# The causal convolution of x in rows: shifted copies by DMA and VectorE products in place of transposes and column taps

## The chip, the cores and the metric

The kernel runs on one NeuronCore of one Trainium2 chip. The metric is device time in microseconds (us) of one launch. The engines are TensorE (PE, its weight loads PEld), VectorE (DVE), ScalarE (ACT), GpSimd (POOL) and SyncE (SP), which here issues nearly all DMAs. Each runs its own instruction stream in order; semaphores join them.

## The reference

One decoder layer over 256 tokens of width 2048 in float32. The part around the change is the Mamba-2 branch (`w_in` gives `z`, `xbc` and others from the normed input):

```
xbc = silu(causal_depthwise_conv(xbc, conv_w, conv_b))   # 4 taps along the tokens
xs, Bm, Cm = split(xbc)                                  # xs: 4096 channels, 64 heads of 64
xdt = xs * dt
y = (C B^T * decay) @ xdt (+ the part over the first 128 tokens, scaled by exp(a_cs))
y = y + d_skip * xs
y = rms_norm_per_512_channels(y * silu(z)) * norm_w
```

Channel c of the convolution at token s is `conv_b[c] + sum over back=0..3 of conv_w[3-back, c] * xbc[s-back, c]`, with zeros in front of token 0. The rest of the layer (differential attention, gates, output projection, SwiGLU) is not touched.

## The kernel before

Tokens lie on the partitions as two tiles of 128 rows (`TT = 2`). Every weight matrix passes through one ring of four buffers in *units* of 256 x 512 weights: SP loads a unit (`load`, L410), ScalarE rounds it to `w_hi` (`split_hi`, L724), VectorE computes the remainder `w_lo = w_raw - w_hi` (`split_lo`, L1257), and TensorE does 12 matmuls of 512 columns on it (`rows_unit`, L2246). ScalarE and VectorE are four units ahead of TensorE: the unit that they call u of a chunk is TensorE's u + 4. ScalarE may round unit n only when TensorE has done unit n-4, because of the ring. A *chunk* is eight units, 512 output columns.

The Mamba-2 stage walks over eight groups of 512 channels. Each group has an x chunk (sum in `acc[0]`) and a z chunk (sum in `acc[1]`). All the other work of the stage is written by hand into the order of the units: `between(u)` on TensorE, and `x_chunk`, `z_chunk` on ScalarE and VectorE, with a number u at each step. The order of one group:

- ScalarE copies the x chunk's sum to rows `x_proj` (L965).
- TensorE, z chunk after u = 0: eight transposes of `x_proj` into `acc[0]`, the matmuls of C and B (L2596), and eight transposes of the former group's `y_row`.
- ScalarE does the first tap and the bias into `conv_x` (four instructions, L838), with channels on the partitions; VectorE adds the other three taps (twelve instructions, L1447) and frees `acc[0]`; ScalarE takes the silu (L995).
- ScalarE, u = 2 and 3: `exps`, eight exponentials each (L977), which waits for masks that GpSimd adds (L2193); VectorE, u = 3 and 4: `decays` (L1658).
- TensorE, z chunk after u = 4: eight transposes of `conv_x` back to rows; VectorE, u = 5: `xdt` and `xdt_end`; ScalarE copies the rows to `y_row` (L1002), GpSimd multiplies them by `d_skip` (L2199).
- TensorE, next x chunk: after u = 1 `y_products` (32 small matmuls of `decay` and `xdt`), after u = 3 `y_rows`. VectorE, u = 3: `tail_gated`; ScalarE, u = 4: squares; GpSimd: reciprocal root; VectorE, u = 6: `tail_normed` (L1624); u = 1 of the z chunk: `tail_transposed` (L1630).

The first group has no former group, and the last group's tail lies in the first two of four gate chunks that follow.

Of the kernel before, what the change touches and what calls it, by code (L numbers as in the profile page):

```python
# [28 lines left out]
ALU = mybir.AluOpType  # L29
# [3 lines left out]
P = 128  # L33
T = 256
# [150 lines left out]
def layer(nc, x, mix_norm_w, w_in, conv_w, conv_b, dt_bias, a_log, d_skip, ssm_norm_w, w_ssm_proj,  # L185
# [3 lines left out]
    with ctx:  # L189
# [6 lines left out]
        def sem(name):  # L196
# [77 lines left out]
        conv_x = at("conv_x", 191, [P, CT, T])  # L274
# [66 lines left out]
        conv_first, conv_done = sem("conv_first"), sem("conv_done")  # L341
        sq_read = sem("sq_read")
        bc_rows_ready, bc_T, x_rows_ready, x_T = sem("bc_rows_ready"), sem("bc_T"), sem("x_rows_ready"), sem("x_T")
# [14 lines left out]
        xs_ready, xs_T, xdt_ready, xrow_ready, skip_ready = (sem(n) for n in (  # L358
            "xs_ready", "xs_T", "xdt_ready", "xrow_ready", "skip_ready"))
# [39 lines left out]
        def _(sp):  # L399
# [302 lines left out]
        def _(act):  # L702
# [232 lines left out]

            def tail_columns(g):
# [4 lines left out]
            def x_chunk(g, head):  # L941
                for u in range(UPC):
                    split_hi()
                    if u == 1 and not head:
                        tail_columns(g - 1)
# [8 lines left out]
                    if u == 4 and not head:  # L954
# [26 lines left out]
            def z_chunk(g, head):  # L981
                for u in range(UPC):
                    split_hi()
                    if u == 0:

                        act.wait_ge(x_T, g + 1)
                        for n in range(CT):
                            last = conv_first_taps(sums(0)[:, n], g * CT, conv_x[:, n], n)
                        last.then_inc(conv_first, 1)
# [27 lines left out]
            for c in range(4):  # L1017
                for u in range(UPC):
                    split_hi()
                    if c == 0 and u == 1:  # L1020
                        tail_columns(G - 1)
                    if c == 0 and u == 4:
# [1791 lines left out]
```

## Time and profile before

| | us |
|---|---|
| three runs, median (lowest to highest) | 2051.03 (2051.0 to 2053.92) |
| the profiled execution | 2051.72 |
| its span | 2050.1 |
| TensorE busy in the span | 2040.8 |
| VectorE, ScalarE, GpSimd busy | 1566.3, 1172.0, 171.6 |

A span runs from the first to the last instruction. Times in rows count from the span's start. The eight groups' x and z chunks lie between about 592 and 998 us. A matmul's busy time includes its pipeline's depth, so matmuls that follow each other overlap in the profile.

### The profile page before, as it was taken

To read this page: it belongs to the slowest core of one execution; us is meant where nothing else is said; L and a number is where in the kernel's file an instruction comes from. 1 tells how busy PE (TensorE), PEld (TensorE's weight loads), DVE (VectorE), ACT (ScalarE), POOL (GpSimd) and SP (SyncE) were. 2 spreads that over 40 slices of the span, in tenths; PEclk is the share of its full clock that TensorE was granted. 3 is DMA by queue.
4 is the path that set the end of the run, shared out by engine and by line. 5 is a ranking of instruction groups with operands and counts; after the bars stand their busy time and mean duration, and the time that the engine had idled before them with its cause. 6 is when DMAs were issued, how large, how long until landed. Compare 5 with 4: busy or idle time off the path is not lost.

```text
span 2050.1 us, 28075 instructions
## 1 busy us (share of the span) xinstructions
PE 2040.8 (100%) x9580; PEld 1677.7 (82%) x9580; DVE 1566.3 (76%) x1861; ACT 1172.0 (57%) x1496; POOL 171.6 (8%) x195
## 2 busy tenths in 40 slices
PE   9999999999999999999999999999999999999999
PEld 8888877778888888888888888888888888887887
DVE  6777866665856777777667887888898889877866
ACT  5444655555556666666655554556666666645543
POOL 1121000000011222222000000010000000000000
PEclk9999999999999999999999999999999999999999
DMA  7656675654566666666565657598888888667574
GB/s 250 199 182 203 188 220 166 176 162 152 182 204 186 185 185 184 185 190 187 167 192 183 212 168 238 177 307 244 258 254 237 250 259 250 196 205 232 176 246 154
DMA packets 220626, 419.80 MB, mean 205 GB/s; under 512 B 16449, under 2 KB 22002, under 8 KB 220290
## 3 DMA queue, kind: packets, MB, share of 16 engines
q1 hardware_dynamic: 212162, 399.48, 61.8%
q0 software_dynamic: 7776, 18.94, 4.4%
q8 instruction: 47, 0.77, 0.2%
q10 hardware_dynamic: 608, 0.34, 0.1%
q14 instruction: 33, 0.27, 0.0%
HBM read 410.25 MB, written 4.26 MB: 202 GB/s over the span
## 4 chain that ended last, share of the span: by engine, by line
PE 92%; DVE 3%; DMA 2%; ACT 1%; issue 0%; SPq 0%; DVEq 0%; ACTq 0%
PE acc L2246 72%; PE side L2333 8%; PE acc L2333 6%; PE side L2262 3%; DMA w_raw<-in_w_ffn_down 1%; DVE w_lo L2038 1%; PE side L2402 1%; PE side L2549 1%; DVE w_raw L1953 0%; ACT w_hi L1216 0%; DVE w_lo L1257 0%; DMA x_row<-in_x 0%; DMA w_raw<-in_w_in 0%; PE acc L2262 0%; ACT w_hi L724 0%
## 5 line engine op out<-in xcount | busy, mean ns | idle before, releaser
L1257 DVE TENSOR_TENSOR w_lo<-w_raw,w_hi 128x1024 fp32r<-128x1024 f32 x332 | 420.7, 1280 | 245.7 <-ACT w_hi L724 244.5
L724 ACT ACTIVATE w_hi<-w_raw 128x1024 fp32r<-128x1024 f32 x332 | 348.5, 1057 | 355.7 <-PE acc L2246 315.2
L2246 PE MATMUL acc<-w_hi,h_hi 128*128 128x512 f32 x1248 | 498.7, 400 | 0.2
L2246 PE MATMUL acc<-w_hi,h_lo 128*128 128x512 f32 x1248 | 487.0, 390 | 0.0
L2246 PE MATMUL acc<-w_lo,h_hi 128*128 128x512 f32 x1248 | 485.9, 389 | 0.0
L2246 PEld LDWEIGHTS acc<-w_hi,h_hi 128*128 128x128 f32 x1248 | 234.4, 188 | 52.7 <-issue 7.0
L2246 PEld LDWEIGHTS acc<-w_hi,h_lo 128*128 128x128 f32 x1248 | 234.3, 188 | 50.3
L2246 PEld LDWEIGHTS acc<-w_lo,h_hi 128*128 128x128 f32 x1248 | 234.7, 188 | 47.6 <-issue 1.9
L1932 DVE TENSOR_TENSOR w_lo<-w_raw,w_hi 128x1024 fp32r<-128x1024 f32 x136 | 165.1, 1220 | 38.0 <-ACT w_hi L1137 35.4
L1053 ACT ACTIVATE w_hi<-w_raw 128x1024 fp32r<-128x1024 f32 x110 | 116.6, 1061 | 117.2 <-PE acc L2246 70.2
L1137 ACT ACTIVATE w_hi<-w_raw 128x1024 fp32r<-128x1024 f32 x136 | 142.9, 1057 | 65.8 <-PE acc L2246 50.4
L1216 ACT ACTIVATE w_hi<-w_raw 128x1024 fp32r<-128x1024 f32 x102 | 107.8, 1060 | 106.5 <-DMA w_raw<-in_w_ffn_down 57.4
L1734 DVE TENSOR_TENSOR w_lo<-w_raw,w_hi 128x1024 fp32r<-128x1024 f32 x110 | 132.2, 1223 | 47.3 <-ACT w_hi L1053 45.4
L1137 ACT ACTIVATE w_hi<-side_raw 128x1024 fp32r<-128x1024 f32 x100 | 106.2, 1062 | 98.1 <-PE acc L2246 45.2
L2038 DVE TENSOR_TENSOR w_lo<-w_raw,w_hi 128x1024 fp32r<-128x1024 f32 x102 | 122.6, 1223 | 47.9 <-ACT w_hi L1216 46.8
L2246 PE MATMUL acc<-w_hi,x2T_hi 128*128 128x512 f32 x384 | 150.9, 393 | 0.5 <-DVE w_lo L1932 0.5
L2246 PE MATMUL acc<-w_hi,x2T_lo 128*128 128x512 f32 x384 | 149.6, 389 | 0.0
L2246 PE MATMUL acc<-w_lo,x2T_hi 128*128 128x512 f32 x384 | 149.4, 389 | 0.0
L1932 DVE TENSOR_TENSOR w_lo<-side_raw,w_hi 128x1024 fp32r<-128x1024 f32 x100 | 122.1, 1221 | 18.3 <-ACT w_hi L1137 16.6
L2246 PE MATMUL acc<-w_hi,a_hi 128*128 128x512 f32 x252 | 98.2, 390 | 0.0
L2246 PE MATMUL acc<-w_hi,a_lo 128*128 128x512 f32 x252 | 98.1, 389 | 0.0
L2246 PE MATMUL acc<-w_lo,a_hi 128*128 128x512 f32 x252 | 98.1, 389 | 0.0
(436 smaller groups left out, 3445.9 us busy)
## 6 DMA issues: line engine op xcount, KB each, us to landing
w_raw<-in_w_in SPq DMA_DIRECT2D x320, 512.0 KB, 4.3
w_raw<-in_w_ffn_down SPq DMA_DIRECT2D x88, 512.0 KB, 4.9
w_raw<-in_w_ffn_gate SPq DMA_DIRECT2D x68, 512.0 KB, 4.6
w_raw<-in_w_ffn_up SPq DMA_DIRECT2D x68, 512.0 KB, 5.2
w_raw<-in_w_ssm_proj SPq DMA_DIRECT2D x64, 512.0 KB, 4.4
side_raw<-in_w_ffn_up SPq DMA_DIRECT2D x40, 512.0 KB, 4.7
w_raw<-in_w_attn_proj SPq DMA_DIRECT2D x32, 512.0 KB, 3.7
w_raw<-in_w_out SPq DMA_DIRECT2D x32, 512.0 KB, 4.7
```

Of the source, the lines that this page charges most:

```text
L724: nc.scalar.activation(w_hi[:, r], w_raw[:, n % RING], ACT.Copy).then_inc(hi_ready, 1)
L1053: nc.scalar.activation(w_hi[:, unit.slot % RING], w_raw[:, source], ACT.Copy).then_inc(hi_ready, 1)
L1137: nc.scalar.activation(w_hi[:, unit.slot % RING], ffn_source(names, name), ACT.Copy).then_inc(hi_ready, 1)
L1216: nc.scalar.activation(w_hi[:, unit.slot % RING], w_raw[:, source], ACT.Copy).then_inc(hi_ready, 1)
L1257: nc.vector.tensor_tensor(w_lo[:, r], w_raw[:, n % RING], w_hi[:, r].bitcast(F32), ALU.subtract).then_inc(lo_ready, 1)
L1734: nc.vector.tensor_tensor(w_lo[:, r], w_raw[:, source], w_hi[:, r].bitcast(F32), ALU.subtract).then_inc(lo_ready, 1)
L1932: nc.vector.tensor_tensor(w_lo[:, r], ffn_source(names, names[n]), w_hi[:, r].bitcast(F32), ALU.subtract).then_inc(lo_ready, 1)
L2038: nc.vector.tensor_tensor(w_lo[:, r], w_raw[:, source], w_hi[:, r].bitcast(F32), ALU.subtract).then_inc(lo_ready, 1)
L2246: done = nc.tensor.matmul(acc[p][:, t], a[:, k0 + kk, cut], w[:, r, kk], start=first and kk == n == 0, stop=last and kk == UK - 1 and n == ...
L2262: return nc.tensor.transpose(out_at, in_, ident)
L2333: done = nc.tensor.matmul(out_at, a, w[:, r, kk], start=first and kk == n == 0, stop=last and kk == UK - 1 and n == 2, skip_group_check=se ...
L2402: last = nc.tensor.matmul(side[:, 1 + m, first:first + width], qkT[half, 0, q * P:(q + 1) * P], qkT[half, 1, 0:width], start=True, stop=True)
```

## The change

The convolution stays in rows. After the x chunk ScalarE writes `x_proj` and frees `acc[0]` at once. SP then issues nine DMAs from `x_proj` to three tiles `earlier[0..2]`, the rows 1, 2 and 3 tokens back: of 112 rows each, of the 15, 14 and 13 rows in front, and of the 1, 2 and 3 rows that wrap from the first tile of tokens to the second. They stand in front of the z chunk's last weight load. GpSimd loads the taps and the bias of a group, broadcast to all partitions (`taps_b` 1 MB, `conv_bias_b` 256 KB). VectorE does four multiplications and four additions of 128x1024 (u = 2 to 5 of its z chunk), and ScalarE's silu follows at its u = 6, in place. Both sets of eight transposes per group, the column taps and the copy to `y_row` go. `taps_b` lies where `decay` lies, so the first half of `exps` waits for `taps_read`, too. `exps` moves from u = 2, 3 to 4, 5; `decays` from 3, 4 to 6, 7; `x_scaled` from u = 5 of the z chunk to u = 0 of the next x chunk; `y_products` and `y_rows` one unit later (2 and 4); `tail_gated` and the squares one unit later; `tail_normed` from VectorE (u = 6 of the x chunk) to ScalarE (u = 0 of the z chunk); the y transposes and `tail_transposed` one unit later. GpSimd multiplies by `d_skip` from `x_proj` before it adds the next group's masks.

```diff
@@ block.sync
-                chunk(w_in, (i + i) * (CW // 2) + COL_Z)
+                for u in range(UPC):
+                    if u == UPC - 1:
+                        sp.wait_ge(x_rows_ready, i + 1)
+                        for back in range(1, TAPS):
+                            sp.dma_start(earlier[back - 1][16:P], x_proj[16 - back:P - back]).then_inc(shift_in, 16)
+                        for back in range(1, TAPS):
+                            sp.dma_start(earlier[back - 1][back:16], x_proj[0:16 - back]).then_inc(shift_in, 16)
+                            sp.dma_start(earlier[back - 1][0:back, 1], x_proj[P - back:P, 0]).then_inc(shift_in, 16)
+                    load(w_in, u * UK, (i + i) * (CW // 2) + COL_Z)
@@ block.scalar
+            def conv_silu(g):
+                act.wait_ge(conv_ready, g + 1)
+                nc.scalar.activation(x_proj[:], x_proj[:], ACT.Silu).then_inc(xs_ready, 1)
+            def tail_normed(g):
+                act.wait_ge(y_rstd, g + 1)
+                for t in range(TT):
+                    last = nc.scalar.activation(y_row[:, t], y_row[:, t], ACT.Copy, scale=y_scale[:, t:t + 1])
+                last.then_inc(y_ready, 1)
...
                 chunk_done()
+                if not head:
+                    act.wait_ge(xdt_ready, g)
+                    act.wait_ge(skip_ready, g)
                 for t in range(TT):
                     last = nc.scalar.activation(x_proj[:, t], acc[0][:, t], ACT.Copy, scale=x_rstd[:, t:t + 1])
                 last.then_inc(x_rows_ready, 1)
+                act.wait_ge(x_rows_ready, g + 1)
+                nc.scalar.sem_inc(acc_free[0], 1)
             def exps(g, hf, head):
                 act.wait_ge(acs_masked, g * 2 + (hf + 1))
+                if hf == 0:
+                    act.wait_ge(taps_read, g + 1)
...
-                    if u == 2:
-                        act.wait_ge(conv_done, g + 1)
-                        nc.scalar.activation(conv_x[:], conv_x[:], ACT.Silu).then_inc(xs_ready, 1)
-                        exps(g, 0, head)
-                    if u == 3:
-                        exps(g, 1, head)
-                    if u == 5:
-                        act.wait_ge(xdt_ready, g + 1)
-                        nc.scalar.activation(y_row[:], side[:, 2:4], ACT.Copy).then_inc(xrow_ready, 1)
+                    if u == 0 and not head:
+                        tail_normed(g - 1)
+                    if u in (4, 5):
+                        exps(g, u - 4, head)
+                    if u == 6:
+                        conv_silu(g)
@@ block.vector
+            def by_taps(tile, back):
+                return nc.vector.tensor_tensor(tile[:], tile[:], taps_b[:, TAPS - 1 - back].unsqueeze(1).broadcast_to([P, TT, CW]), ALU.mult)
+            def conv_step(g, u):
+                if u == 2:
+                    dve.wait_ge(shift_in, g * 144 + 144)
+                    dve.wait_ge(taps_in, g * 32 + 32)
+                    by_taps(earlier[0], 1)
+                    by_taps(earlier[1], 2)
+                if u == 3:
+                    by_taps(earlier[2], 3)
+                    by_taps(x_proj, 0).then_inc(taps_read, 1)
+                if u == 4:
+                    dve.wait_ge(taps_read, g + 1)
+                    nc.vector.tensor_tensor(earlier[0][:], earlier[0][:], earlier[1][:], ALU.add)
+                    link(nc.vector.tensor_tensor(x_proj[:], x_proj[:], earlier[2][:], ALU.add))
+                if u == 5:
+                    link(nc.vector.tensor_tensor(x_proj[:], x_proj[:], earlier[0][:], ALU.add))
+                    nc.vector.tensor_tensor(x_proj[:], x_proj[:], conv_bias_b[:].broadcast_to([P, TT, CW]), ALU.add).then_inc(conv_ready, 1)
...
+            def x_chunk(g, head):
+                for u in range(UPC):
+                    split_lo()
+                    if not head:
+                        tail_step(g - 1, u)      # u == 0: x_scaled, u == 4: tail_gated
+            def z_chunk(g, head):
+                for u in range(UPC):
+                    split_lo()
+                    if u == 2 and not head:
+                        tail_transposed(g - 1)
+                    conv_step(g, u)
+                    if u in (6, 7):
+                        decays(g, u - 6)
@@ block.gpsimd, for each group i
                 pool.wait_ge(decay_exp, i * 2 + 2)
                 loads(i + 1)
+                skip(i, first)
+                pool.wait_ge(y_sum, i + 1)
+                taps_load(i + 1)
                 tail(i)
-                group(i + 1)
+                masks(i + 1)
@@ block.tensor
-                    if u == 1:
+                    if u == 2:
                         y_products(g)
-                    if u == 3:
+                    if u == 4:
                         y_rows(g)
...
                     if u == 0:
-                        pe.wait_ge(x_rows_ready, g + 1)
-                        for n in range(CT):
-                            for t in range(TT):
-                                at_col = (n % 2) * T + t * P
-                                last = transpose(acc[0][:, n // 2, at_col:at_col + P], x_proj[:, t, n * P:(n + 1) * P])
-                        last.then_inc(x_T, 1)
...
-                        if not first:
-                            y_columns(g - 1)
-                    if u == 4:
-                        pe.wait_ge(xs_ready, g + 1)
-                        if not first:
-                            pe.wait_ge(yT_ready, g)
-                        for n in range(CT):
-                            for t in range(TT):
-                                last = transpose(side[:, 2 + t, n * P:(n + 1) * P], conv_x[:, n, t * P:(t + 1) * P])
-                        last.then_inc(xs_T, 1)
+                    if u == 1 and not first:
+                        y_columns(g - 1)
+                    if u == 4 and not first:
+                        pe.wait_ge(yT_ready, g)
```

## Rows read from the trace of the kernel before

**Rows 1.** The page: span, TensorE's busy time, chain that ended last by engine.

```profile
span 2050.1 us, 28075 instructions
PE 2040.8 (100%) x9580; PEld 1677.7 (82%) x9580; DVE 1566.3 (76%) x1861; ACT 1172.0 (57%) x1496; POOL 171.6 (8%) x195
PE 92%; DVE 3%; DMA 2%; ACT 1%; issue 0%; SPq 0%; DVEq 0%; ACTq 0%
```

**Rows 2.** Waits, 614 to 1024 us: who waited for whom, us, times, longest us.

```profile
DVE w_lo L1257 <- ACT w_hi L724: 104.3, 66, 5.0
ACT w_hi L724 <- DMA w_raw<-in_w_in: 16.3, 7, 2.9
PE side L2262 <- DVE y_row L1624: 0.7, 1, 0.7
```

**Rows 3.** Chain of one group, in order of time: start us, us, what.

```profile
769.19 0.87 PE acc L2262 x8
770.07 0.43 PE side L2596 x2
770.72 0.87 PE side L2262 x8
771.60 10.91 PE acc L2246 x48
782.50 0.87 PE side L2262 x8
...
796.99 1.90 PE side L2549 x32
...
819.95 0.88 PE acc L2262 x8
```

**Rows 4.** ScalarE's timeline in the same group: start us, us, instruction, idle before.

```profile
777.10 1.06 ACT L724 ACTIVATE w_hi<-w_raw 128x1024 fp32r<-128x1024 f32 x1 [1.28 <-PE acc L2246]
778.07 1.04 ACT L995 ACTIVATE conv_x<-conv_x 128x1024 f32<-128x1024 f32 x1
779.13 1.28 ACT L977 ACT_TABLE_LOAD   x1
780.42 2.46 ACT L977 ACTIVATE decay<-acs_b,neg_acs 128x128 f32<-128x128 f32 x8
782.78 1.04 ACT L724 ACTIVATE w_hi<-w_raw 128x1024 fp32r<-128x1024 f32 x1
783.73 2.44 ACT L977 ACTIVATE decay<-acs_b,neg_acs 128x128 f32<-128x128 f32 x8
...
796.12 1.27 ACT L1005 ACTIVATE z_row<-acc,small 128x512 f32<-128x512 f32 x2
797.89 2.01 ACT L724 ACTIVATE w_hi<-w_raw 128x1024 fp32r<-128x1024 f32 x2 [0.51 <-ACT z_row L1005]
```

**Rows 5.** VectorE's timeline in the same group.

```profile
778.71 1.21 DVE L1630 TENSOR_TENSOR yT<-side,cols 128x1024 f32 x1
779.84 1.21 DVE L1257 TENSOR_TENSOR w_lo<-w_raw,w_hi 128x1024 fp32r<-128x1024 f32 x1
783.86 1.23 DVE L1257 TENSOR_TENSOR w_lo<-w_raw,w_hi 128x1024 fp32r<-128x1024 f32 x1 [2.81 <-ACT w_hi L724]
785.00 1.22 DVE L1658 TENSOR_TENSOR decay<-decay,cb 128x1024 f32<-128x1024 f32 x1
...
790.57 1.28 DVE L1682 TENSOR_TENSOR xdt<-side,dt 128x512 f32<-128x512 f32 x2
791.97 0.69 DVE L1690 TENSOR_TENSOR xdt_end<-xdt,edge 128x512 f32<-128x512 f32 x1
793.89 3.31 DVE L1257 TENSOR_TENSOR w_lo<-w_raw,w_hi 128x1024 fp32r<-128x1024 f32 x2 [1.23 <-ACT w_hi L724]
```

**Rows 6.** GpSimd's timeline in the same group.

```profile
793.09 3.03 POOL L2199 TENSOR_TENSOR y_row<-y_row,d_skip_b 128x512 f32<-128x512 f32 x2 [23.61 <-ACT y_row L1002]
```

**Rows 7.** SP's issues of `qk_row`, the copies between SBUF tiles (256 KB).

```profile
L481 SPq DMA_DIRECT2D qk_row<-qk x16: 627/630/1347, 264.5 to 459.8; - x16
DMA to landing us min/median/max: 3.7/4.8/5.5
```

**Rows 8.** One group's stretch: busy time of each engine, clock, DMA share, GB/s.

```profile
767.00:818.00 51.00, 51.00 (x265) 42.24 (x264) 38.01 (x41) 33.07 (x52) 11.53 (x10) 1.00 0.60 184
```

More of the change, by code:

```diff
@@ L273, in layer @@
         x_proj = at("x_proj", 187, [P, TT, CW])
-        conv_x = at("conv_x", 191, [P, CT, T])
+        earlier = [at(f"earlier{n + 1}", kb, [P, TT, CW]) for n, kb in enumerate((138, 142, 175))]
+        taps_b = at("taps_b", 167, [P, TAPS, CW])
+        conv_bias_b = at("conv_bias_b", 191, [P, 1, CW])
         y_row = at("y_row", 195, [P, TT, CW])
@@ L943, in x_chunk @@
                     split_hi()
-                    if u == 1 and not head:
+                    if u == 2 and not head:
                         tail_columns(g - 1)
@@ L953, in x_chunk @@
                         nc.scalar.activation(edge[:].rearrange("p t h -> p (t h)"), side[:, 3, 0:TT * HS], ACT.Exp).then_inc(edge_ready, 1)
-                    if u == 4 and not head:
+                    if u == 5 and not head:
                         tail_squares(g - 1)
@@ L1602, in _ @@
                 nc.vector.tensor_tensor(gated, acc[c % 2][:], gated, ALU.mult).then_inc(acc_free[c % 2], 1)
+            for back in range(1, TAPS):
+                last = nc.vector.memset(earlier[back - 1][0:back, 0], 0.0)
+            link(last)
             def tail_gated(g):
@@ L1632, in tail_transposed @@
                                         ALU.mult).then_inc(yT_ready, 1)
-            def x_chunk(g, head):
-                for u in range(UPC):
-                    split_lo()
-                    if not head:
-                        if u == 3:
-                            tail_gated(g - 1)
-                        if u == 6:
-                            tail_normed(g - 1)
-            def conv_taps(g, back):
-                for n in range(CT):
-                    last = conv_other_taps(sums(0)[:, n], g * CT, conv_x[:, n], n, back)
-                if back < TAPS - 1:
-                    link(last)
-                else:
-                    last.then_inc(conv_done, 1)
             def decays(g, hf):
@@ new lines, in x_scaled @@
+            def x_scaled(g):
+                by_head = "p (h d) -> p h d"
+                dve.wait_ge(xs_ready, g + 1)
+                for t in range(TT):
+                    last = nc.vector.tensor_tensor(
+                        xdt[:, t].rearrange(by_head, d=HP), x_proj[:, t].rearrange(by_head, d=HP),
+                        dt[:, t, bass.ds(g * HG, HG)].unsqueeze(2).broadcast_to([P, HG, HP]), ALU.mult)
+                last.then_inc(xdt_ready, 1)
+                dve.wait_ge(xdt_ready, g + 1)
+                nc.vector.tensor_tensor(
+                    xdt_end[:].rearrange(by_head, d=HP), xdt[:, 0].rearrange(by_head, d=HP),
+                    edge[:, 0, bass.ds(g * HG, HG)].unsqueeze(2).broadcast_to([P, HG, HP]), ALU.mult).then_inc(xdt_end_ready, 1)
@@ L1662, in z_chunk, with tail_step @@
+            def tail_step(g, u):
+                if u == 0:
+                    x_scaled(g)
+                if u == 4:
+                    tail_gated(g)
+            def x_chunk(g, head):
                 for u in range(UPC):
                     split_lo()
-                    if u == 0:
-                        dve.wait_ge(conv_first, g + 1)
-                        for back in range(1, TAPS):
-                            conv_taps(g, back)
-                    if u == 1 and not head:
-                        tail_transposed(g - 1)
@@ L2205, in _, with next_group @@
             pool.dma_start(acs_dram[:], acsT[:]).then_inc(acs_out, 16)
+            taps_load(0)
             pool.wait_ge(acs_out, 16)
             loads(0)
-            group(0)
-            with repeat(pool, G - 1, [(own, 2)]) as i:
+            masks(0)
+            def next_group(i, first=False):
                 pool.wait_ge(decay_exp, i * 2 + 2)
                 loads(i + 1)
+                skip(i, first)
+                pool.wait_ge(y_sum, i + 1)
+                taps_load(i + 1)
                 tail(i)
-                group(i + 1)
+                masks(i + 1)
+            next_group(0, True)
+            with repeat(pool, G - 2, [(own, 2)]) as i:
+                next_group(i + 1)
+            skip(G - 1)
             tail(G - 1)
```

81 lines of the change are left out of this document (28 added, 53 removed).

## The prediction

> **What bounds the kernel now.** I read the page first: TensorE is busy 2040.8 of 2050.1 us and holds 92% of the chain that ended last [rows 1]. Then the waits of the stretch that the change touches: from 614 to 1024 us TensorE waits once, 0.7 us, while VectorE waits 104.3 us for ScalarE's roundings [rows 2]. So the other engines have slack, and a group costs what TensorE's instructions cost. The chain of one group gives the period: the x transposes start at 769.19 and again at 819.95, 50.76 us apart [rows 3]. A unit of 12 matmuls is 10.91 / 4 = 2.73 us, each set of eight transposes is 0.87 us, the C and B matmuls from 770.07 to 770.72 are 0.65 us, and the products of `decay` and `xdt` 1.90 us [rows 3]. The question is thus twofold: what TensorE is spared, and whether the rest can still be done in the time of a shorter group.
>
> **What TensorE is spared.** Two sets of eight transposes per group, at 769.19 and 782.50, 0.87 us each [rows 3]: 1.75 us per group, 14.0 us over eight. They are on the path. The other sets stay. With nothing late, a group is 50.76 - 1.75 = 49.0 us.
>
> **What the other engines get.** VectorE loses twelve column taps and `tail_normed` and gets eight operations of 128x1024 from SBUF. No multiplication by a broadcast tap is in the trace; `decays` is the same shape and has a broadcast operand, 1.22 us, and at most 1.14 from one start to the next (783.86 to 785.00) [rows 5]. From below I take the two-operand 512-wide operation, 1.28 for two [rows 5], which is no cheaper; nothing in the rows halves it. So 8 x 1.14 = 9.1 us. VectorE is busy 38.0 of 51 us in a group now [rows 8]; the sum of busy time is no problem after either. The order is.
>
> **The chain through the new order.** Call 0 the moment when TensorE ends the x chunk. Its z units end at 2.73; then C and B, 0.65; z1; the y transposes, 0.87; z2 ends at 3 x 2.73 + 1.52 = 9.7; the z chunk at 8 x 2.73 + 1.52 = 23.4; the next chunk's unit 2 at 31.5, and there `y_products` waits for `decays` and `xdt`. Now the other way round, from 9.7, when ring buffer z6 comes free:
> - ScalarE starts to round z6; VectorE's `w_lo` starts 1.08 after it (782.78 to 783.86 [rows 4, 5]), at 10.9. Behind it VectorE has no pause: `w_lo` z6, `tail_transposed`, two products, `w_lo` z7, two products: 7 x 1.14 (778.71 to 779.84, 783.86 to 785.00 [rows 5]) = 8.0. `taps_read` at 18.9.
> - `exps` is ready for its first half at 16.2 but has the new wait for `taps_read`, since the taps lie under `decay`. Queued behind it on ScalarE are the roundings of every later unit, the silu and the z rows. From 19.0: table 1.29, eight exponentials 2.36 (780.42 to 782.78), rounding 0.95, exponentials 2.35, rounding 0.97 (777.10 to 778.07): 26.9 [rows 4]. VectorE's additions are done at about 27.2, beside the next table load.
> - Table 1.29, silu 1.06 (778.07 to 779.13), rounding 0.97, z rows 1.27 and 0.50 to the next rounding (796.12 to 797.89) [rows 4]: 32.0. Only now is the unit rounded behind whose `w_lo` the new place of `x_scaled` lies: 1.08, `w_lo` 1.14, `xdt` 1.40 (790.57 to 791.97 [rows 5]): `xdt` is there at 35.6.
>
> TensorE wants it at 31.5, so it stands 4.1 us per group, behind a wait that before had `xdt` done at 791.97 for products at 796.99, 5 us early [rows 3, 5]. `y_products` is one unit later than before, which is in the 31.5; its input is some ten us later. To this comes GpSimd: its `d_skip` products (3.03 us for two) run against `w_lo`, and the two `w_lo` take 3.31 instead of 2 x 1.14 or so [rows 5, 6]. In the new order these products start after the silu, at 29.3, just where `decays`, `w_lo` and `xdt` stand. I add from 0 to 1.0, and take 0.5: 4.6 us.
>
> The Trainium skill's page "SBUF — State Buffer" (Who interferes with whom) says that a VectorE instruction with two SBUF inputs contends with a GpSimd instruction that reads SBUF, one with a single SBUF input doesn't. The 3.31 us agree [rows 5]. By it the old taps, with one input in PSUM, were free of it, and all eight new operations and `xdt` are not; the sum by it is the upper end of that term, 5.1 us.
>
> **The shifted rows.** SP waits for `x_rows_ready` at 2.3 and then issues nine DMAs. By the copies of `qk_row` an issue takes 0.63 us, and landing 3.7 to 5.5, median 4.8 [rows 7]: the last is issued at 8.0 and lands at 12.8. VectorE comes for them at 10.9 + 2 x 1.14 = 13.2. Just in time, by 0.4. The big ones hold 448 KB where `qk_row` has 256, but they are issued first. I count 0, and up to 2 us per group if they land later. The last weight load of the z chunk waits behind them; it is issued at 8.1 and wanted at 12.5, and a few us of lateness are covered by the ring (TensorE comes to it at 20.6). The DMA engines are busy 0.60 at 184 GB/s [rows 8], 9.4 MB in 51 us; 1.5 MB of rows and 1.3 MB of taps make it 12.2 MB, about 0.75 of a 53.6 us group. ScalarE's waits for weights, seven of 2.3 us [rows 2], grow, but don't reach TensorE as long as they stay under 5 us. GpSimd's taps load and masks have the whole x chunk, and cost nothing on the path.
>
> `tail_normed` moves to ScalarE, u = 0: its rows are ready at 5.2, and the y transposes come at 6.1. Close, but 0. In the first gate chunks, where no exponentials are queued, I count 0.5 once.
>
> **The sum.** 8 x (4.6 - 1.75) + 0.5 = 23.3 us. The profiled execution took 2051.72 (span 2050.1 and 1.6 around it), 0.7 above the median of 2051.03; on the profile it is 2075.0, on the median 2074.3. I say 2074.
>
> **The rivals.**
> 1. *The transposes come off and no wait takes their place.* For it: 104.3 us of VectorE's waits [rows 2], and a ring four deep. It has one place, the wait of `y_products` for `xdt`, and is decided at 1.75 us per group: below that the kernel is faster. The chain would have to be 2.9 us shorter. That takes the products by taps at half my value (2 us, four of them ahead of `taps_read`) and a table load that runs while `taps_read` is awaited (1.29), and no loss to GpSimd. With all of that the stall is 0.8 and the time 2051 - 8 x 0.95 = 2043; with none at all 2051 - 14 = 2037. Against it: every link is a row, and they follow each other on in-order engines.
> 2. *The shifted rows decide.* If they land 2 us late, VectorE stands at u = 2 and everything behind it moves on: 8 x 2 more, 2090. With 4 us it is 2106. For it: 0.4 us of slack and a fuller queue. Against it: the small copies should land faster than `qk_row`.
> 3. *ScalarE's table loads cost more in the chain.* In the rows a load is 1.28 us, and the next instruction starts 1.29 after its start [rows 4]. If each of the two loads in the chain dragged another 1.4 us, the stall would be 7.4 and the time 2096. The Trainium skill's page "ScalarE: Activation LUTs" (What ACT_TABLE_LOAD costs) gives 1283 ns and a drain of about 1380 ns for each switch, an estimate of 2 x 1.38 on top; the rows show no drain, so I give it little.
> 4. *The two cancel*, a stall of 1.5 to 2.1 us: 2049 to 2054.
>
> **Chances.** The forecast 0.74, rival 1 0.08, rival 2 0.12, rival 3 0.03, rival 4 0.03. A measurement of this kernel tells about 0.2%, 4 us, from no change. Faster 0.07, same 0.04, slower 0.89. The forecast's own range: the table load during the wait and no GpSimd loss, 2.8 per group, 2060; GpSimd's full loss and a little of rival 2, 6 per group, 2085. For 8 in 10 I reach down to 2056 and up to 2092.
>
> **What would show it.** Right: TensorE's waits name `xdt` (VectorE) eight times, 3 to 6 us each, some 37 us in all; the period of a group is 53.6; ScalarE's first exponentials wait for VectorE about 2.7 us per group (at 16.2 they are ready); the transposes of `x_proj` and `conv_x` are gone, 16.6 us of busy time. Wrong: TensorE's waits stay near 1 us and the period is 49; or they name `w_lo`, which would put it on the shifted rows or the weights; or a product by taps takes well under 1.1 us; or the transposes that go leave less than 1.75 us per group.

## The result, and the profile after

The changed kernel takes 2100.24 us (median of 4 runs, 2099.48 to 2102.64), the kernel before, run beside it, 2051.28: a ratio of 1.0238, interval 1.022 to 1.0255. It is slower by 49 us. Forecast were 2074 with 2056 to 2092 as the range, so the sign was right and the size not: the change costs twice what was said.

TensorE's waits in the stretch that [rows 2] show for before, here 614 to 1080 us (who waited for whom: us in all, times, longest):

```profile
DVE w_lo L1281 <- ACT w_hi L735: 136.8, 79, 7.4
ACT w_hi L735 <- DMA w_raw<-in_w_in: 51.6, 25, 5.8
PE side L2595 <- DVE xdt L1690: 31.3, 7, 4.5
ACT y_cols L962 <- PE side L2595: 30.1, 8, 5.0
ACT L1009 <- DVE x_proj L1666: 13.8, 7, 2.5
DVE earlier L1666 <- DMA earlier<-x_proj: 8.1, 5, 2.8
PE acc L2292 <- DVE w_lo L1281: 7.2, 12, 1.8
PE side L2595 <- issue: 4.4, 1, 4.4
```

Before, TensorE waited 0.7 us here. Now it waits 31.3 + 4.4 = 35.7 us at `y_products`, eight times, and for `xdt` as forecast (36.8). Two lines were not in the forecast: 7.2 us for `w_lo` in twelve places, and 51.6 us in which ScalarE waits for weights, 16.3 before. Eleven of the twelve waits are for one of the two units that ScalarE rounds behind its exponentials. In the group shown next ScalarE starts these roundings at 920.83 and 924.12, and TensorE resumes at 923.19 and 926.72:

```profile
920.83 1.04 ACT L735 ACTIVATE w_hi<-w_raw 128x1024 fp32r<-128x1024 f32 x1
924.12 1.05 ACT L735 ACTIVATE w_hi<-w_raw 128x1024 fp32r<-128x1024 f32 x1
923.19 0.50 PE L2292 MATMUL acc<-w_hi,h_hi 128*128 128x512 f32 x1 [0.70 <-DVE w_lo L1281]
926.72 0.50 PE L2292 MATMUL acc<-w_hi,h_hi 128*128 128x512 f32 x1 [0.49 <-DVE w_lo L1281]
```

So most of these waits hang on the same chain as the wait for `xdt`.

The chain of waits through one group, in order of time (start, us, what), answers to [rows 3]:

```profile
897.40 1.25 ACT x_proj L992 x2
898.68 0.58 SPq L496
...
905.27 0.81 SPq L498
906.12 5.01 DMA earlier<-x_proj
...
913.53 1.22 DVE w_lo L1281
...
915.80 1.23 DVE x_proj L1666
...
921.88 2.34 ACT decay L1009 x8
924.21 0.95 ACT w_hi L735
...
926.48 1.06 ACT x_proj L950
...
932.96 1.22 DVE xdt L1690 x2
934.22 3.68 PE side L2595 x32
937.90 6.42 PE acc L2292 x24
```

Follow it from the top: the copy of the x chunk, the nine copies of rows on SP, their landing, the products by taps, the exponentials, the silu, `xdt`, and only then TensorE. The last lines hold a cost that no part of the forecast names. `y_products` takes 3.68 us here; the same 32 matmuls took 1.90 in [rows 3]. The 24 matmuls behind it take 6.42 us, 0.27 each, where four units of them took 10.91 / 48 = 0.23 [rows 3]. The windows of that stretch say why (stretch, us, busy us of TensorE, its weight loads, VectorE, ScalarE, GpSimd with counts, then granted clock, DMA share, GB/s):

```profile
932.00:933.00 1.00, 0.00 (x0) 0.00 (x0) 1.00 (x2) 0.24 (x1) 0.00 (x0) 0.82 0.89 342
933.00:934.00 1.00, 0.00 (x0) 0.00 (x0) 1.00 (x2) 0.43 (x1) 0.00 (x0) 0.50 0.19 72
...
938.00:939.00 1.00, 1.00 (x3) 0.81 (x4) 0.00 (x0) 0.97 (x1) 0.00 (x0) 0.50 0.88 317
939.00:940.00 1.00, 1.00 (x5) 0.83 (x4) 0.00 (x0) 0.00 (x0) 0.00 (x0) 0.76 1.08 352
940.00:941.00 1.00, 1.00 (x6) 0.78 (x6) 0.00 (x0) 0.00 (x0) 0.00 (x0) 1.00 0.73 281
600.00:1060.00 460.00, 417.01 (x1977) 338.95 (x1977) 318.04 (x270) 252.90 (x384) 99.53 (x81) 0.95 0.75 216
```

TensorE stood idle from 929.74 to 934.22. During that wait the granted clock fell to 0.50, the 1.2 GHz level, and it stayed there for the first 5 us of the work that followed. Each wait of 4.5 us is thus paid twice: 1.7 us more in `y_products`, about 1 in the matmuls behind it. Over the stage the clock was 0.95, where it was 1.00 in [rows 8]. The Trainium skill's page "TensorE: Matmul & The Clock Gate" ("HAM oscillation — how this bites in real kernels") describes this pattern: behind a wait that recurs, each burst of matmuls starts at the half clock. The trace agrees: all eight `y_products` of the changed kernel take 3.09 to 3.68 us. The forecast had not weighed it.

The profile pages of the two kernels give an account. The span grew by 48.5 us, from 2050.1 to 2098.6. TensorE is idle for 51.7 us of it instead of 9.3, 42.4 more: the two waits (35.7 and 7.2, less the 0.7 of before). And it is busy for 2046.9 us instead of 2040.8, although 14.0 us of transposes are gone: 20.1 us more for the same work. Most of the 20.1 is the clock; the first experiment takes 16.3 away. The remaining 4 are mostly a matter of counting, by an estimate: a matmul of 512 columns is 0.39 us long in the profile and the next one starts 0.23 after it, so every stop adds 0.16 us of busy time, 3.3 us for 20 stops.

### The profile page after: what moved, and what is told of

Same layout as the page of the kernel before. It is cut to its first block, busy times and chain, and to the rows that moved or that the text cites. A ratio compares the mean times of both kernels' runs of the same rounds, so it can differ in the third digit from the quotient of the medians.

```text
span 2098.6 us, 27734 instructions
## 1 busy us (share of the span) xinstructions
PE 2046.9 (98%) x9452; PEld 1678.0 (80%) x9452; DVE 1585.2 (76%) x1816; ACT 1158.0 (55%) x1470; POOL 181.2 (9%) x211
## 4 chain that ended last, share of the span: by engine, by line
PE 79%; DVE 6%; ACT 5%; DMA 4%; issue 3%; SPq 3%; ACTq 0%; DVEq 0%
PE acc L2292 59%; PE side L2379 8%; PE acc L2379 6%; PE side L2308 2%; ACT w_hi L735 2%; ACT decay L1009 1%; DMA w_raw<-in_w_in 1%; PE side L2595 1%; SPq L498 1%; DVE w_lo L1281 1%; SPq L496 1%; DMA earlier<-x_proj 1%; SPq L499 1%; PE side L2448 1%; DVE decay L1663 1%
```

## The experiments

Two theories stood at the outset. **The chain:** the new order brings `xdt` late, TensorE waits, and the wait lowers the clock. **The rows:** the nine DMAs and the weights behind them are the cause, by landing late. Each kernel below is the changed one with the edit shown; where it says so, it builds on a former one. All are medians of interleaved runs with the kernel before at 2050.6 to 2052.4.

### The clock: `warm`

```diff
             def y_products(g):
+                for _ in range(16):
+                    nc.tensor.matmul(side[:, 3], h_hi[:, 0, 0:P], h_hi[:, 0:2].rearrange("p k t -> p (k t)"), start=True, stop=True)
                 pe.wait_ge(decay_ready, g * 2 + 2)
```

> The changed kernel with 16 extra matmuls of 128x512 (on values that nobody reads) in front of TensorE's wait for y_products' inputs, 3.6 us at full clock, less than the 4.5 us that it waits there; the layer's output is not touched. Theory (clock): the waits of 36 us at y_products are as forecast, and what lies above the forecast is mostly TensorE at 1.2 instead of 2.4 GHz for some us after each wait (y_products 3.68 instead of 1.90 us). The extra matmuls keep it at 2.4: about 16 to 20 us come back, 2080 to 2085, with y_products at 1.9 us and the granted clock at 1.00. Rival (crowded DMAs: late weights and shifted rows): the time stays at 2100 or rises.

Measured: 2083.98 us (2083.24 to 2086.34), ratio 1.0167 (1.015 to 1.0184). TensorE's timeline at the same place (start, us, instruction, and in brackets the idle time before it):

```profile
921.23 3.79 PE L2586 MATMUL side<-h_hi 128*128 128x512 f32 x16
925.88 1.97 PE L2596 MATMUL side<-decay,xdt 128*64 128x128 f32 x32 [0.86 <-DVE xdt L1690]
```

Useless work of 3.79 us in the wait, and `y_products` is back at 1.97 us; nothing else was touched. 16.3 us of the 49 are the clock. The pages agree: without this filler, 8 x 3.79 = 30.3 us in all, TensorE is busy 2061.0 - 30.3 = 2030.7 us, 16.2 less than in the changed kernel.

### The chain: `early_xdt`, `half_taps`, `best1`

`early_xdt` takes a unit of rounding out of the way of `xdt`; `half_taps` lets the first exponentials start when two of the four products by taps are done; `best1` has both.

```diff
# early_xdt, VectorE, z chunk (x_scaled at u = 0 of the x chunk goes)
-                    if u in (6, 7):
-                        decays(g, u - 6)
+                    if u == 6:
+                        decays(g, 0)
+                        decays(g, 1)
+                    if u == 7:
+                        x_scaled(g)
# half_taps, ScalarE and VectorE
-                if hf == 0:
-                    act.wait_ge(taps_read, g + 1)
+                act.wait_ge(taps_read if hf else taps_half, g + 1)
...
                 if u == 2:
-                    by_taps(earlier[0], 1)
-                    by_taps(earlier[1], 2)
+                    by_taps(earlier[2], 3)
+                    by_taps(earlier[1], 2).then_inc(taps_half, 1)
                 if u == 3:
-                    by_taps(earlier[2], 3)
+                    by_taps(earlier[0], 1)
                     by_taps(x_proj, 0).then_inc(taps_read, 1)
```

> VectorE's order alone: both decays at u = 6 and x_scaled at u = 7 of the z chunk, ahead of the w_lo of the next x chunk's unit 4. Forecast's theory (the chain to xdt sets the wait at y_products): xdt is done about 2.7 us earlier, the wait falls from 4.5 to about 1.8 us per group, 22 us. With the clock theory the shorter wait also leaves the clock at 2.4 GHz and gives up to 18 more: 2060 to 2066. Rival (the DMAs): the waits shift to w_lo and at most 10 us are gained, 2090.

> The products by taps are done in the order 3 back, 2 back, 1 back, 0 back; the first two use the half of taps_b that lies under the first half of decay, so the first exponentials wait for two products instead of four, the second ones for all four. Theory: the 2.4 us that ScalarE waits there go out of the chain to xdt; the wait at y_products falls to about 2.2 us; 18 us, and with the clock held some 16 more: 2064 to 2070, or 2082 if the clock still falls. Rival (the DMAs set it, the wait for taps is covered): under 8 us.

> early_xdt and half_taps together. Theory: nothing waits at y_products any more, TensorE is spared its transposes, 14 us: 2037 plus the waits for w_lo of up to 7 us: 2037 to 2046, faster than before the change. Rival (the DMAs): the late weights and rows still cost 10 to 20 us: 2050 to 2060.

Measured: `early_xdt` 2087.87 (ratio 1.0188, 1.0171 to 1.0205), `half_taps` 2087.23 (1.0182, 1.0165 to 1.0199), `best1` 2072.06 (1.0109, 1.0092 to 1.0125). TensorE's waits for `xdt` with them, the first line of each kernel:

```profile
PE side L2596 <- DVE xdt L1690: 22.9, 7, 3.3
```

```profile
PE side L2593 <- DVE xdt L1688: 28.6, 7, 4.4
```

```profile
PE side L2594 <- DVE xdt L1688: 22.4, 7, 3.3
```

With the eighth wait of each (3.3, 4.0, 2.8) these are 26.2, 32.6 and 25.2 us, for 35.7 in the changed kernel. The profile of `early_xdt` is of its fastest run, 2082.7. The sign is that of the chain, each edit alone is worth 12 to 13 us, together 28. `half_taps` gains more beside that wait than in it: the waits for `w_lo` fall from 7.2 to 2.4 us, and TensorE's busy time from 2046.9 to 2040.8. `early_xdt` came out near its rival's 2090, but the waits did not shift to `w_lo` (5.3 us) as that rival said. All three expectations were far too good. The links that I had shortened were replaced by others, and VectorE's timeline of `best1` shows one of them:

```profile
910.38 3.20 DVE L1661 TENSOR_TENSOR decay<-decay,cb 128x1024 f32<-128x1024 f32 x2
913.50 2.06 DVE L1279 TENSOR_TENSOR w_lo<-w_raw,w_hi 128x1024 fp32r<-128x1024 f32 x1
915.49 1.28 DVE L1688 TENSOR_TENSOR xdt<-x_proj,dt 128x512 f32<-128x512 f32 x2
```

GpSimd ran its `d_skip` products beside them:

```profile
910.61 3.87 POOL L2233 TENSOR_TENSOR y_row<-x_proj,d_skip_b 128x512 f32<-128x512 f32 x2 [1.93 <-ACT x_proj L950]
```

The two `decay`, `w_lo` and `xdt` start at 910.38, 913.50 and 915.49, so `xdt` starts 5.11 us after `decay`, where three pitches of 1.14 are 3.42: GpSimd costs the chain 1.7 us in this order, not the 0.5 of the forecast, and its own two go from 3.03 [rows 6] to 3.87. The Trainium skill's page "SBUF — State Buffer" (Who interferes with whom) says that a VectorE instruction with two SBUF inputs contends with a GpSimd instruction that reads SBUF. The trace agrees; the forecast had cited this rule and then taken half.

### `best1` with a full clock: `best1_warm`

The edit is that of `warm`, on `best1`.

> best1 with 16 matmuls of 128x512 more ahead of the wait of the products (their result is not used), which fill it. In the kernel of the change this edit gave 16.3 us although the matmuls take 3.5 us a group themselves. In best1 the waits are 3.3 us at most, 25 in all, and the products take 2.5 us on average for 1.97. If the clock in the products' stretch is what the rest of the loss is, filling gives back what lies between 2.5 and 1.97 and the units just behind, 4 to 8 us, and costs nothing beyond the wait it fills but up to 0.5 us in groups whose wait was shorter than the matmuls: 2064 to 2072. Rival, the clock no longer matters at waits this short: 2072 to 2078.

Measured: 2068.1 (1.0086, 1.0071 to 1.0102), 4.0 under `best1`. That is net. The filler takes 30.3 us where the waits had taken 25.2, and TensorE's busy time without it falls from 2036.4 to 2056.4 - 30.3 = 2026.1 us. So at waits of 2.8 to 3.3 us the clock and the stops still cost `best1` some 10 us, and my rival that the clock no longer matters there is wrong. It does not fall every time: `y_products` takes 1.97 us in three of the eight groups of `best1` and 2.45 to 3.38 in five.

### The copies of rows: `no_shift`, `load_first`

`no_shift` leaves out the nine DMAs; the taps 1 to 3 back are multiplied by zeros. `load_first` puts the weight load that stands behind them in front of them.

```diff
# no_shift
-                        sp.wait_ge(x_rows_ready, i + 1)
-                        for back in range(1, TAPS):
-                            sp.dma_start(earlier[back - 1][16:P], x_proj[16 - back:P - back]).then_inc(shift_in, 16)
...
-                    dve.wait_ge(shift_in, g * 144 + 144)
+                    dve.wait_ge(x_rows_ready, g + 1)
# load_first
+                    load(w_in, u * UK, (i + i) * (CW // 2) + COL_Z)
                     if u == UPC - 1:
                         sp.wait_ge(x_rows_ready, i + 1)
...
-                    load(w_in, u * UK, (i + i) * (CW // 2) + COL_Z)
```

> The changed kernel without the nine DMAs per group and without the waits for them; the products use tiles of zeros, so the taps 1 to 3 back are left out of the result. Theory (three terms on top of each other): the shifted rows came 1.6 us late for VectorE and the weights behind them up to 5 us late for ScalarE. Without them the products start 1.6 us earlier, the wait at y_products falls to about 2.9 us, the waits for w_lo (7 us in all) go, and part of the clock's loss with them: 2072 to 2082. Rival (the DMAs are all that is above the forecast): 2074 minus 14 or less, below 2065. Rival (they cost nothing): 2100.

> The changed kernel with the z chunk's last weight load in front of the nine DMAs instead of behind them. If the late weights set the chain, 8 to 15 us are gained: 2085 to 2092. If the shifted rows and the wait for the taps set it, as in the chain of the changed kernel, the rows come 0.4 us later and it is 2097 to 2104.

Measured: `no_shift` 2087.54 (1.0179, 1.0162 to 1.0196), `load_first` 2109.95 (1.0284, 1.0267 to 1.0301). The waits of `no_shift`, then those of `load_first`:

```profile
PE side L2590 <- DVE xdt L1685: 29.2, 7, 4.5
ACT w_hi L730 <- DMA w_raw<-in_w_in: 7.1, 8, 1.4
PE side L2590 <- issue: 4.4, 1, 4.4
PE acc L2287 <- DVE w_lo L1276: 0.6, 1, 0.6
```

```profile
DVE earlier L1666 <- DMA earlier<-x_proj: 24.4, 8, 6.6
PE acc L2292 <- DVE w_lo L1281: 17.6, 19, 2.0
```

Without any DMA for rows TensorE still waits 33.6 us for `xdt`: the rows are not the cause of that wait, since both ends of it move together. I had expected it to fall to 2.9 us per group, and its longest is still 4.5. But the rows are worth 12.7 us: 6.6 in the waits for `w_lo` (7.2 to 0.6), 3.8 in TensorE's busy time (2046.9 to 2043.1) and 2.1 in the waits for `xdt`. And with the rows one weight load later the kernel loses 9.7 us. VectorE waits 24.4 us for them in `load_first`, 8.1 before that edit: 2.0 more per group, where I had expected 0.4. ScalarE's waits for weights fell there, from 51.6 to 41.8, while TensorE's for `w_lo` rose from 7.2 to 17.6, so late weights are not what makes these. The rows thus decide when the chain starts, though not everywhere: in the changed kernel's first four groups the chain of waits runs through the weight load that SP issues behind the nine copies, in the last four through the rows. In the third group:

```profile
738.10 3.65 DMA w_raw<-in_w_in
```

### The transposes put back as idle work: `transposes`

```diff
+            def idle_transposes():
+                for n in range(CT):
+                    for t in range(TT):
+                        at_col = (n % 2) * T + t * P
+                        transpose(acc[0][:, n // 2, at_col:at_col + P], h_hi[:, n, t * P:(t + 1) * P].bitcast(F32))
...
                     if u == 0:
+                        pe.wait_ge(x_rows_ready, g + 1)
+                        idle_transposes()
...
+                    if u == 4:
+                        idle_transposes()
```

> The changed kernel with both sets of eight transposes back in their places on TensorE, on values that nobody reads (the first behind the wait for x_proj's rows, as before). Theory: TensorE waits at y_products anyway, so the second set is absorbed and the first, ahead of unit z2 from which the chain starts, costs 0.9 us per group: 2104 to 2110, and a shorter idle time may give some of it back through the clock. Rival (what TensorE is spared counts in full): 2114.

Measured: 2095.71 (1.0223, 1.0206 to 1.024), 4.5 under the changed kernel by the medians and 3 by the ratios, although TensorE does 14 us more. The waits for `xdt` fell from 35.7 to 30.4 and those for `w_lo` from 7.2 to 1.0:

```profile
PE side L2595 <- DVE xdt L1690: 26.7, 7, 4.2
PE side L2595 <- issue: 3.7, 1, 3.7
PE acc L2292 <- DVE w_lo L1281: 1.0, 1, 1.0
```

In the changed kernel the 14 us that were spared on TensorE are worth nothing: it mostly arrives earlier at waits that end no earlier. Part of it is the clock again: TensorE's busy time is 2053.0 - 14.0 = 2039.0 without the idle work, for 2046.9, and three of the eight `y_products` take 1.97 us. I had expected 2104 to 2110.

### Removing the waits: `best2`, `best1_skip`, `best1_split`, `best3`

`best2` is `best1` with two edits. (skip) GpSimd's `d_skip` products wait until `xdt_end` is done. (split) The nine DMAs go out by tap, with a semaphore for each, and the weight load before the last three.

```diff
# skip, GpSimd
-                pool.wait_ge(xs_ready, g + 1)
+                pool.wait_ge(xdt_end_ready, g + 1)
# split, SP (VectorE waits for shift_by[back - 1] ahead of each product)
+                        for back in (3, 2, 1):
+                            if back == 1:
+                                load(w_in, u * UK, (i + i) * (CW // 2) + COL_Z)
+                            sp.dma_start(earlier[back - 1][16:P], x_proj[16 - back:P - back]).then_inc(shift_by[back - 1], 16)
...
```

> early_xdt and half_taps, with the shifted rows in three sets of own semaphores (3 back first, then 2, the last weight load, then 1), so that the first products wait for three DMAs only, and GpSimd's d_skip products behind xdt_end so that they don't run against decays, w_lo and xdt. Theory: in early_xdt plus half_taps 3.3 us per group are left, of which GpSimd's products cost VectorE 1.9 and the late rows and weights 3; without both no wait is left and the clock holds: 2038 to 2048, below the kernel before. Rival: another link takes over with 1 to 2 us per group: 2050 to 2062.

> best1 with one edit of best2 alone: GpSimd's d_skip products wait for xdt_end and not for the silu, so they no longer run beside decays, w_lo and xdt. Theory that the shared port carries most of what best1 still loses: in best1 the two decays, w_lo and the two xdt there took about 3.20 + 2.06 + 1.9 where 2.4 + 1.2 + 1.3 are the prices alone, some 2 us a group; the waits for xdt fall from 25 to about 9, and the clock stays up with them: 2072.1 - 16 to 20 = 2052 to 2058. Rival, that the late rows and weights carry it: 2068 to 2072.

> best1 with the other edit of best2 alone: the nine DMAs in the order 3 back, 2 back, the last weight load, 1 back, with a semaphore of their own each. Theory that the shared port carries most: 2066 to 2071 (rows come 1 us earlier at most). Rival, late rows and weights: 2054 to 2060. If the two edits add up, the gains of best1_skip and of this one are 22.4 us together; if the clock makes them more than additive (each shortens a wait that is either long enough to cost the clock or not), their sum is less than 22.4.

Measured: `best2` 2049.68 (0.9998, 0.9988 to 1.0007), `best1_skip` 2052.85 (1.0012, 1.0002 to 1.0021), `best1_split` 2064.3 (1.0062, 1.0044 to 1.0081). Moving GpSimd's products out of the way gives 19.2 us, the order of the DMAs 7.8, both 22.4: they overlap. What is 1.7 us a group in the rows is worth 2.4, since it also ends the half clock (1.00 in the stage of `best1_skip`, 0.98 in `best1`).

`best3` moves `y_products` and the tail behind it one unit later, so that no wait for `xdt` is left:

```diff
                 def between(u):
-                    if u == 2:
+                    if u == 3:
                         y_products(g)
-                    if u == 4:
+                    if u == 5:
                         y_rows(g)
# and with them: y_cols u = 2 to 3, tail_gated u = 4 to 5, the squares u = 5 to 6
```

> best2, and the products of decay and xdt, the rows of y and the tail behind them each one unit later in the next x chunk (TensorE u = 3 and 5, ScalarE's copy of the columns u = 3, VectorE's tail_gated u = 5, ScalarE's squares u = 6). In best2 TensorE still waited 8.6 us for xdt (eight times, at most 1.6). My theory (the chain to xdt against the place of the products, and nothing else): one unit more is 2.7 us, so the wait for xdt is 0 and the time is 2049.7 - 8.6 = 2041, with 2038 to 2044 as the range; 14 us under the transposes' kernel less 4 for what is left. Rival: the tail that now starts a unit later (y_gated, squares, reciprocal root, tail_normed at u = 0 of the z chunk) becomes the new wait, for y_row at the y transposes, 1 to 2.5 us a group: 2049 to 2060.

Measured: 2056.72 (1.0025, 1.0014 to 1.0035), slower than `best2`, where I had expected 2041. The wait for `xdt` was gone as expected, and another stood in its place, which is not the one that my rival named:

```profile
ACT w_hi L738 <- DMA w_raw<-in_w_in: 91.9, 42, 5.6
PE acc L2296 <- DVE w_lo L1282: 15.6, 22, 1.5
```

### The DMAs once nothing else is in the way: `best3_no_nine`, `best3_taps_once`, `best3_neither`

The first leaves out the nine copies (as `no_shift`), the second the load of the taps after group 0 (VectorE multiplies by rows of `bc`; the bias is still loaded), the third both.

> best3 without the nine DMAs and the waits for them; VectorE multiplies tiles of zeros (the taps 1 to 3 back are left out of the result). best3 has no wait for xdt left, but TensorE waits 15.6 us for w_lo in 22 places and ScalarE 91.9 us for weights, where before had 16.3. Theory A: the nine copies delay the weight loads (a load issued between them landed 9.2 us after its issue, where 3.8 was the median before). Without them ScalarE waits less than 35 us for weights, TensorE's waits for w_lo fall below 4, and the time is 2056.7 - 12 to 16 = 2041 to 2045. Theory B, the 1.25 MB of taps and bias per group: only some 4 us come back, 2052. Theory C, VectorE's and ScalarE's own order (table loads and exponentials ahead of roundings) makes w_lo late, DMAs or not: 2053 to 2057.

> best3 with the taps loaded for the first group alone; VectorE multiplies by other rows in their place (the result has other taps), the bias is still loaded. 1 MB less per group of DMA. Theory A (the nine copies delay the weights): 2052 to 2057. Theory B (bandwidth as a whole, DMA busy 0.82 of the time in this stretch): most of the 15.6 us of waits for w_lo go, 2041 to 2047. Theory C (the engines' order): 2053 to 2057.

> Both at once: neither the nine copies nor the taps after the first group. If the DMAs, whichever, are what stands between best3 and the 2037 that the spared transposes alone would give, this is 2037 to 2042. If theory C holds it stays above 2050.

Measured: 2036.82 (0.9934, 0.9919 to 0.9949), 2037.56 (0.9932, 0.9917 to 0.9947) and 2036.11 (0.9924, 0.9909 to 0.9939). Either of them alone gives all of it back, so neither the copies nor the bytes of the taps are the cause by themselves; my theory A named the first alone. This is the 2037 of the transposes without any new wait. GpSimd's and SP's timelines of `best3` show that the two meet. The taps' load is issued here

```profile
867.65 0.82 POOL L2220 DMA_DIRECT2D taps_b<-in_conv_w  x1 [7.00 <-PE side L2610]
```

and the first shifted rows at 875.12, 7.5 us later, while taps and bias need 9.5 and 12.1 us (median) to land:

```profile
875.12 0.57 SPq L499 DMA_DIRECT2D earlier<-x_proj  x1
...
879.76 0.40 SPq L413 DMA_DIRECT2D w_raw<-in_w_in  x1
```

The weight load at 879.76 was rounded at 888.93, after ScalarE had waited 5.63 us for it.

### `best4` and `best5`

`best4` is `best3` with that weight load in front of the nine copies. `best5` is `best4` with `y_rows`, `tail_gated` and the squares back at u = 4, 4 and 5; only `y_products` stays at u = 3. GpSimd issues the taps when `y_rows` is done, so their load moves up by a unit.

```diff
# best4, SP
+                        load(w_in, u * UK, (i + i) * (CW // 2) + COL_Z)
                         sp.wait_ge(x_rows_ready, i + 1)
                         for back in (3, 2, 1):
-                            if back == 1:
-                                load(w_in, u * UK, (i + i) * (CW // 2) + COL_Z)
# best5, TensorE
                     if u == 3:
                         y_products(g)
-                    if u == 5:
+                    if u == 4:
                         y_rows(g)
```

> best3 with the z chunk's last weight load back in front of the nine copies. In the kernel of the change this order cost 9.7 us, since the rows decided there; in best3 no wait for xdt is left and the rows have 1.5 to 2.7 us of slack, and the weights are what is late. If late weights at this one place are the cause, 2045 to 2050, faster than before; if the rows come late again (VectorE waits over 2 us a group for them) and push the chain to xdt by more than the slack, 2056 to 2062.

> best4 with y_rows back at u = 4 (and tail_gated at u = 4, the squares at u = 5 with it); y_products stays at u = 3. GpSimd issues the taps when y_rows is done, so their DMA starts a unit earlier: in best3 it was issued 7.5 us before the first shifted row, in best2 9.8, and the taps and bias take 9.5 to 12 us to land. Theory that best4's loss against the 2037 of the kernels with less DMA is this overlap: the taps are in before the nine copies start, ScalarE's waits for weights fall from 55.0 to 35 to 45, TensorE's waits for w_lo from 4.1 to 0 to 2, and the time is 2038 to 2043. Rivals: the overlap doesn't matter, 2044 to 2048; or y_rows, only one unit behind y_products, now waits for ScalarE's copy y_cols, 0.5 to 1 us a group: 2046 to 2052.

Measured: `best4` 2046.08 (0.9973, 0.9963 to 0.9984) and `best5` 2039.26 (2037.33 to 2041.13; 0.9937, 0.9923 to 0.995), 13 us faster than the kernel before and 61 faster than the changed one, with all nine copies and all taps. The waits of `best5`, its stage, and the start of the x chunk's copy in consecutive groups:

```profile
ACT w_hi L737 <- DMA w_raw<-in_w_in: 39.7, 25, 5.9
PE acc L2295 <- DVE w_lo L1281: 1.8, 3, 1.0
```

```profile
600.00:1060.00 460.00, 457.55 (x2253) 375.62 (x2252) 358.81 (x302) 288.65 (x426) 107.17 (x84) 1.00 0.82 241
```

```profile
813.27 1.25 ACT L994 ACTIVATE x_proj<-acc,small 128x512 f32<-128x512 f32 x2
862.27 1.25 ACT L994 ACTIVATE x_proj<-acc,small 128x512 f32<-128x512 f32 x2
911.27 1.25 ACT L994 ACTIVATE x_proj<-acc,small 128x512 f32<-128x512 f32 x2
```

The period is 49.00 us, just what the prediction gave for a group with nothing late. The DMA engines are as busy as in `best3` (0.82 of the time in both), so it was not the amount. That it was the overlap is argued, not shown. In `best5` the taps are issued at 853.73 and the rows at 864.97, 11.2 us apart; in `best4` it is 8.2 (856.05 and 864.25), in `best3` 7.5, in `best2` 9.8, and TensorE's waits for `w_lo` are 1.8, 4.1, 15.6 and 0.9 us. But `best4` also has a weight load in another place, and `best5` has `y_rows` and VectorE's and ScalarE's steps behind it a unit earlier. No run moves the taps' load alone.

## Why the prediction was right or wrong

- **What TensorE is spared, 1.75 us per group.** Right: with nothing late the period is 49.00, and the kernels with fewer DMAs are 13.5 to 15.0 us under before. In the changed kernel the saving is worth nothing (`transposes`).
- **The chain through the new order, a wait of 4.6 us.** Right in place, releaser and size: 4.48 us in the group shown, 35.7 in all for 36.8. The size is luck in part: both of its ends were 2 us off, and the errors cancel. Counted from the end of the x chunk (896.4), the taps were read at 20.6 for 18.9, `xdt` was there at 37.8 for 35.6, and TensorE came at 33.3 for 31.5.
- **What failed: the sum.** "8 x (4.6 - 1.75) + 0.5" prices TensorE's wait at its length. In the rows of before TensorE never stands, so no row there shows what standing costs; I took the durations of `y_products` and of the units from [rows 3], which were all taken at clock 1.00. The missing term measures 16.3 us, by `warm`. With it the sum would have been 2074.3 + 16.3 = 2090.6, inside the range. The 7.2 us of waits for `w_lo`, which the forecast put at nothing, are the next largest part.
- **The shifted rows: "I count 0".** Mis-sized as well. An issue was put at 0.63 us by [rows 7]; the nine took 0.93 each, 8.4 us in all (898.68 to 907.09), and the last rows landed 14.7 us after the chunk's end, not at 12.8. VectorE, forecast at 13.2, stood for them, in five groups by the waits and 1.6 us in the one shown. By `no_shift` the DMAs are worth 12.7 us with what hangs on them. This was rival 2, at 0.12. Its 2 us of lateness happened in the group shown, together with the forecast's own mechanism and not in its place; over the eight groups VectorE stood 8.1 us, 1.0 each. On the weights, ScalarE's waits grew to 51.6 us, and the longest, 5.8, is over the 5 us up to which the forecast had them reach nobody. In the first four groups the late weight load is a link of the chain, but most of the 7.2 us for `w_lo` is for units rounded behind the exponentials, and the forecast had not followed these units to TensorE.
- **GpSimd, 0.5 us per group.** Too low in the shortened kernels: 1.7 in `best1`, where `decays`, `w_lo` and `xdt` stood close together. In the changed kernel the rows show one operation of 2.06 us for 1.22 beside it, 0.8.
- **Products by taps, 1.14 us each.** Right: 1.22 us, one from the next 1.13.
- **Rival 1 (no wait, 2037 to 2043).** Not this kernel, but the number holds for `best5`, after six edits: 2039.
- **Rival 3 (table loads drag).** Wrong: a table load takes 1.28 us and the next instruction starts 1.29 after it (917.18, 918.47 in the timeline of the changed kernel). The exponentials waited for the taps 13.8 + 1.4 us in eight groups, 1.9 each, for 2.7.

Open is the last part of the 20.1 us: between the 16.3 of `warm` and the account some 4 us stay that no single run isolates, and that the stops explain only by an estimate. Open too is why `best5` is faster than `best3` with the same DMAs. Nor did any run take the nine copies' issue time on SP apart from their bytes.

## What to carry over

A wait on TensorE, where it bounds the kernel, has its clock as part of the price, and a trace in which that engine never stands can't show it. A spared instruction is worth its time only if all that the engine waits for next is early as well; putting it back as idle work shows whether it is. And added DMAs are to be placed, not only counted: against 2036 without them the same bytes cost 21 us in one order (`best3`) and 3 in another (`best5`).

## What the hardware showed unexpectedly

- In a wait of 4.48 us TensorE's granted clock fell to 0.50 and stayed there for 5 us of full work after it; 3.8 us of useless matmuls in each wait gained 16.3 us over eight. In `best1` waits of 3.3 us at most still brought half-clock stretches in five groups of eight.
- In `best2`, whose waits for `xdt` are 1.6 us at most, all eight sets of `y_products` ran at the full clock: 256 matmuls of 276 ns each, 15.7 us. In the changed kernel one set took 3.68.
- Copies between SBUF tiles took 0.56 to 0.95 us each to issue in `best5`, 2 KB or 448 KB alike, and up to 1.93 in the changed kernel.
- The taps' load of 1 MB (9.5 us to land) and the nine copies of 1.5 MB together cost 1 us or less each without the other (2037.6 and 2036.8, for 2036.1 without either). With the taps' load issued 7.5 us before the copies, beside the weights' stream, the second of the two costs 19 to 20 us more (2056.7).
